# A sixth expert buffer, a new load order, a pairwise last iteration and a float32 gather in a two-layer transformer step

## What is computed

```python
# hierarchical MoE: top group, then top 2 of its 8 experts; 32 experts of width 256
hid = silu(einsum('bsd,edf->bsef', h, w_gate)) * einsum('bsd,edf->bsef', h, w_up)
hid = hid * combine[..., None]            # zero for experts that a token did not choose
y   = einsum('bsef,efd->bsd', hid, w_down)
x   = layer_norm(ALPHA * x + g2 * y, ln2_g, ln2_b)
```

## Time and profile before

| | |
|---|---|
| median of three runs | 1087.92 us |
| the profiled execution | 1086.85 us |
| its span | 1085.1 us |
| TensorE busy | 967.4 us (89%) |
| VectorE, ScalarE, GpSimd busy | 326.5, 230.6, 39.6 us |
| from HBM | 321.05 MB |
| expert gate and up loads | 64 of 2 MB, median 17.6 us from issue to landing |
| expert down loads | 64 of 1 MB, median 12.9 us |

### The profile page before, as it was taken

How to read it: one execution, slowest core, us unless ns; L and a number is a source line. 1 busy time by engine, 2 the same in 40 slices (tenths; PEclk the granted TensorE clock), 3 DMA queues, 4 the chain that set the end, 5 groups by cost and what they waited for, 6 DMA issues and landing times.

```text
span 1085.1 us, 15639 instructions
## 1 busy us (share of the span) xinstructions
PE 967.4 (89%) x6820; PEld 590.2 (54%) x6820; DVE 326.5 (30%) x744; ACT 230.6 (21%) x475; POOL 39.6 (4%) x60
## 2 busy tenths in 40 slices
PE   3999899998899898978879998999998989897875
PEld 1887758777743333334248876687884333332421
DVE  2112323222851312111170132331276231211215
ACT  2102314200251312111121132241014231211211
POOL 1100000010000000000010000000001000000000
PEclk9899999999999999998989999999999999999998
DMA  9938854586439999999875426766442999999970
GB/s 381 409 141 348 335 224 155 219 318 274 160 132 422 389 427 429 429 427 423 374 304 219 161 63 239 316 272 209 182 174 82 413 428 429 429 430 429 422 310 39
DMA packets 38526, 324.60 MB, mean 299 GB/s; under 512 B 4920, under 2 KB 5048, under 8 KB 9392
## 3 DMA queue, kind: packets, MB, share of 16 engines
q1 hardware_dynamic: 33696, 308.82, 69.6%
q0 software_dynamic: 4320, 13.28, 3.5%
q10 hardware_dynamic: 432, 1.39, 0.3%
HBM read 321.05 MB, written 2.42 MB: 298 GB/s over the span
## 4 chain that ended last, share of the span: by engine, by line
PE 75%; DMA 10%; DVE 6%; ACT 5%; issue 3%; SPq 1%; DVEq 0%; ACTq 0%
PE ps L768 13%; PE ps L666 9%; PE ps L817 8%; PE ps L692 6%; PE ps L872 5%; PE ps L944 5%; PE ps L958 5%; PE ps L781 5%; DMA expert_gate_up<-in_w_gu 4%; DMA expert_down<-in_w_dn 3%; PE ps L595 3%; PE ps L725 2%; PE ps L616 2%; DMA dense<-in_w_ada 2%; PE ps L827 2%
## 5 line engine op out<-in xcount | busy, mean ns | idle before, releaser
L768 PE MATMUL ps<-expert_gate_up,gathered_prompt 128*32 128x512 f32 x768 | 172.4, 603 | 5.0 <-ACT gathered_sample L1143 2.3
L768 PE MATMUL ps<-expert_gate_up,gathered_sample 128*32 128x512 f32 x768 | 172.4, 603 | 0.0
L817 PE MATMUL ps<-expert_down,hiddenT 128*32 128x512 f32 x1024 | 117.5, 602 | 11.8 <-ACT gathered_sample L1143 4.5
L666 PE MATMUL ps<-hT,dense 128*128 128x256 f32 x512 | 115.9, 385 | 0.0
L768 PEld LDWEIGHTS ps<-expert_gate_up,gathered_prompt 128*32 128x32 f32 x768 | 49.8, 111 | 115.6 <-issue 112.9
L666 PEld LDWEIGHTS ps<-hT,dense 128*128 128x128 f32 x512 | 97.4, 192 | 16.1 <-issue 2.8
L1557 DVE SCALAR_TENSOR_TENSOR y_lo<-ps,slot_weight,y_hi 128x512 fp32r<-128x512 f32 x64 | 48.1, 751 | 105.7 <-ACT y_hi L1175 105.6
L817 PEld LDWEIGHTS ps<-expert_down,hiddenT 128*32 128x32 f32 x1024 | 32.0, 110 | 82.8 <-issue 57.4
L1540 DVE TENSOR_TENSOR hidden<-hidden,ps 128x256 f32<-128x256 f32 x32 | 13.4, 420 | 194.0 <-ACT hidden L1159 194.0
L692 PE MATMUL ps<-dense,hT 128*128 128x256 f32 (+1 forms) x320 | 69.3, 381 | 1.7 <-ACT hT L1100 1.7
L692 PEld LDWEIGHTS ps<-dense,hT 128*128 128x128 f32 x320 | 60.6, 201 | 10.4 <-ACT hT L1100 2.5
(11 more groups left out here) (217 smaller groups left out, 1110.1 us busy)
## 6 DMA issues: line engine op xcount, KB each, us to landing
expert_gate_up<-in_w_gu SPq DMA_DIRECT2D x64, 2048.0 KB, 17.6
expert_down<-in_w_dn SPq DMA_DIRECT2D x64, 1024.0 KB, 12.9
dense<-in_w_ada SPq DMA_DIRECT2D x48, 1024.0 KB, 9.1
dense<-in_w_in SPq DMA_DIRECT2D x28, 1024.0 KB, 9.3
dense<-in_w_o SPq DMA_DIRECT2D x8, 1024.0 KB, 6.3
dense<-in_w_out SPq DMA_DIRECT2D x8, 1024.0 KB, 5.1
dense<-in_w_c SPq DMA_DIRECT2D x4, 1024.0 KB, 24.6
gate<-ada_rows POOLq DMA_DIRECT2D x4, 1024.0 KB, 8.5
```

Of the source, the lines that this page charges most:

```text
L666: last = mm(b[:, m * 256:(m + 1) * 256], w[:, k, m * P:(m + 1) * P], hT[:, k, :], start=(k == 0), stop=(k == KD - 1))
L768: last = mm(ps[r0:r0 + 32, q, :], xg[s][:, k, at_:at_ + CAP], w_gu[(i * EPI + 2 * q + j) % SLOTS][:, k, :], start=(k == 0), stop=(k == KD ...
L817: last = mm(ps[32 * e:32 * e + 32, banks[c], :], h, w_dn[(i * EPI + e) % SLOTS][:, f, c * 512:(c + 1) * 512], start=(f == 0), stop=(f == 1 ...
```

## The change

- A sixth expert buffer lies in the memory that held `h_hi` and `h_lo` (gate and up) and, for down, in that of `h2T`. Expert e lies in buffer e % 6, except 26 (buffer 5) and 29 (buffer 2). `gate2` and `ln2` move to the memory of buffer 5's gate and up part.
- The gather multiplies `xh2` itself by a float32 selection matrix, one matmul where there were two; `h_hi` and `h_lo` and their semaphores go.
- `gather_pair` uses banks 2, 3, 0, 1, and so also waits for the copies of `hiddenT` and `selectT` out of banks 0 and 1.
- The last iteration is done pairwise, as the middle ones; the down matmuls of request 1 are in two halves around the scatter of request 0, and VectorE's and ScalarE's programs follow.
- SP loads expert 5's gate and up after the attention (once `z_ready` is complete), its down part after expert 4's, then the others in a new order. `g2` and `ln2` are issued by SP behind the last expert.
- The first 15 dense loads of each layer go to other units (`FIRST_UNITS`).

```diff
-SLOTS = 5
+SLOTS = 6
+GATHER_BANK = (2, 3, 0, 1)
-FIRST_UNITS = (6, 7, 8, 9, 10, 12, 13, 0, 1, 3, 4, 11, 14, 2, 5)
+FIRST_UNITS = (9, 10, 11, 12, 13, 6, 7, 0, 1, 3, 4, 14, 8, 2, 5)
+BUFFER = [e % SLOTS for e in range(NE)]
+BUFFER[26], BUFFER[29] = 5, 2
...
# SP: load order
                     if (kind, i) == ("ada", gap_ada(l)[0] + 3):
+                        sp.wait_ge(z_ready, 8 * (l + 1))
+                        gate_up_load(l, M[l], 5)
                         first_gate_up(l, 3)
                         first_down(l, 3)
...
-                for e in range(5, EPI * 2):
-                    main_load(l, e)
-                for e in range(5, EPI * 2):
-                    main_down(l, e)
-                for i in range(2, ITERS):
-                    ...
+                k, v = nth(l, ("route", 1))
+                sp.wait_ge(filled[k], v + 1)
+                down_load(l, M[l], 5)
+                for e in range(6, 22, 4):
+                    for part in (e, e + 1, e + 2):
+                        main_load(l, part)
+                    for part in (e, e + 1):
+                        main_down(l, part)
+                    main_load(l, e + 3)
+                    for part in (e + 2, e + 3):
+                        main_down(l, part)
+                for e in (22, 23):
+                    main_load(l, e)
+                for e in (22, 23):
+                    main_down(l, e)
+                ... (the branch, then 24 and 25 in the same way)
+                for e in range(26, NE, 2):
+                    main_load(l, e)
+                    main_load(l, e + 1)
+                    main_down(l, e)
+                    main_down(l, e + 1)
+                sp.wait_ge(*reached(M[l], "h_filled", expert_pass(26)))
+                sp.wait_ge(ada_stored, 32 * (2 * l + 2))
+                load_rows(sp, l, 5, g2, post2_in)
+                load_ln(sp, l, "ln2", ln2, post2_in)
...
# TensorE: gather
-                    for hp, part in enumerate((h_hi, h_lo)):
-                        last = mm(ps[:, bank, at_ * CHUNK:(at_ + 1) * CHUNK], part[:, s, k * P:(k + 1) * P],
-                                  sel[:, n % 2, s, :], start=(hp == 0), stop=(hp == 1))
+                    last = mm(ps[:, bank, at_ * CHUNK:(at_ + 1) * CHUNK], xh2[:, s, k * P:(k + 1) * P],
+                              sel[:, n % 2, s, :], start=True, stop=True)
...
# TensorE: last iteration
-                gate_up_request(m, i, 0, 0, range(0, 8))
-                for s in range(2):
-                    scatter(m, i - 1, i - 1, s, False)
-                turn_request(m, i, 0, 0)
-                down(m, None, i, i, 0, (2, 3), False, ITERS + 1)
-                gate_up_request(m, i, 1, 1, range(0, 4))
-                scatter(m, i, i, 0, False)
-                gate_up_request(m, i, 1, 1, range(4, 8))
-                turn_request(m, i, 1, 1)
-                pe.wait_ge(*reached(m, "lo_done", 4 * i + 2))
-                down(m, None, i, i, 1, (2, 3), False, ITERS + 2)
-                scatter(m, i, i, 1, False)
+                for q in range(2):
+                    gate_up_pair(m, None, i, q)
+                    scatter(m, i - 1, i - 1, q, False)
+                turn_pairs(m, i)
+                down(m, None, i, i, 0, (2, 3), True, i + 2)
+                down(m, None, i, i, 1, (2, 3), True, i + 2, (0,))
+                scatter(m, i, i, 0, False)
+                down(m, None, i, i, 1, (2, 3), True, i + 2, (1,))
+                scatter(m, i, i, 1, False)
...
# VectorE: last iteration
-                hidden_product(m, i, 0, 0)
+                for q in range(2):
+                    hidden_product(m, i, q, q)
                 for c in range(2):
                     low(m, i, i, 0, c, 2 + c)
+                low(m, i, i, 1, 0, 2)
                 moe_sum(l, 0)
+                low(m, i, i, 1, 1, 3)
                 moe_residual(l, 0)
                 e = row_sums(y_sum, 0, 8, LN_EPS)
-                hidden_product(m, i, 1, 1)
                 centre(y_sum, ln2, 0)
-                low(m, i, i, 1, 0, 2)
                 scale(e, ln2, 0, 8, x2_ready, l)
-                low(m, i, i, 1, 1, 3)
```

More of the change, by code:

```diff
@@ L64 @@
 GAP_UNITS = (13, 14, 15, 12)
+BUFFER = [e % SLOTS for e in range(NE)]
+BUFFER[26], BUFFER[29] = 5, 2
+IN_BUFFER = [[e for e in range(NE) if BUFFER[e] == j] for j in range(SLOTS)]
 SMALL_LOADS = 6
@@ L363, in expert_pass, with load_rows, load_ln @@
             i = e // EPI
-            return 2 * i + 2 if i in (0, ITERS - 1) else 2 * i + (e % EPI) // 2 + 1
+            return 2 * i + 2 if i == 0 else 2 * i + (e % EPI) // 2 + 1
         def landed(r, e):
-            return 16 * (e // SLOTS + 1) if r is None else r * (16 * len(range(e % SLOTS, NE, SLOTS))) + 16 * (e // SLOTS + 1)
+            held = IN_BUFFER[BUFFER[e]]
+            n = 16 * (held.index(e) + 1)
+            return n if r is None else r * (16 * len(held)) + n
         def dram(ap, offset, dims):
             return bass.AP(ap.tensor, offset, dims)
+        def load_rows(eng, l, part, out, s):
+            src = dram(io["ada"], (l * 2 * ADA + part) * D, [[0, P], [ADA * D, 2], [1, D]])
+            eng.dma_start(out[:, :, :], src).then_inc(s, 16)
+        def load_ln(eng, l, name, out, s):
+            for j, n in enumerate((name + "_g", name + "_b")):
+                eng.dma_start(out[:, j, :], dram(io[n], l * D, [[0, P], [1, D]])).then_inc(s, 16)
         block = ctx.enter_context(nc.Block())
@@ L383, in dense_load @@
                 elif l and b < 15:
-                    e = max(range(b // 3, NE, SLOTS))
+                    e = IN_BUFFER[b // 3][-1]
                     if b % 3 < 2:
@@ L488, in store_rows @@
                     pool.dma_start(io["ada"][l, c, g], ada_row[c:P:32, :]).then_inc(ada_stored, 16)
-            def load_rows(l, part, out, s):
-                src = dram(io["ada"], (l * 2 * ADA + part) * D, [[0, P], [ADA * D, 2], [1, D]])
-                pool.dma_start(out[:, :, :], src).then_inc(s, 16)
-            def load_ln(l, name, out, s):
-                for j, n in enumerate((name + "_g", name + "_b")):
-                    pool.dma_start(out[:, j, :], dram(io[n], l * D, [[0, P], [1, D]])).then_inc(s, 16)
             def bias4_load(l, a, b):
@@ L800, in turn_request, with down @@
                 last.then_inc(w["hidT_filled"], 1)
-            def down(w, r, g, i, s, banks, paired, turns):
+            def down(w, r, g, i, s, banks, paired, turns, halves=(0, 1)):
                 if s == 0 or not paired:
                     for e in range(i * EPI, i * EPI + EPI):
-                        pe.wait_ge(*reached(w, "dn_in", landed(r, e), e % SLOTS))
+                        pe.wait_ge(*reached(w, "dn_in", landed(r, e), BUFFER[e]))
                     pe.wait_ge(*reached(w, "hidT_copied", turns))
-                for c in range(2):
+                for c in halves:
                     if paired and s:
```

118 lines of the change are left out of this document (54 added, 64 removed).

## The result

Four runs of the changed kernel took 1075.45, 1075.65, 1078.43 and 1080.28 us, median 1077.04; four of the kernel before took 1087.81 to 1088.95, median 1088.04. The ratio is 0.9909 [0.9891, 0.9926]: 8 to 12 us faster, where the forecast was 1083.2 us and its range began at 1079. Six more runs of the changed kernel later took 1079.12 to 1081.98 us (ratio 0.9935 [0.9915, 0.9955]); the median of all ten is 1080.2 us, against 1087.2 us for 59 runs of the kernel before. So the gain is nearer 7 than 11 us, and three us of the miss lie in which four runs came first: the six later ones all lie within the forecast's range.

A forecast was written before the change was run, and what follows sets the result against it. TensorE and the weight loads were taken to bound the kernel neck and neck. First layer +0.35 and second -5.0 gave -4.7 us: 1082.2 us profiled, 1083.2 us median; own range 1080.5 to 1086, wider range 1079 to 1089.

The forecast's parts named there:

- the price of the gathers: Float32 matmuls at 0.44 us: request 0's gather +0.5 (first layer) and 0, request 1's +1.1 us in each layer.
- the clock recovers further: Rival: request 0's gather has a hole shorter by 0.7 us and half clock behind it may not come; about 1080; chance 0.17.
- The closings: After down of iteration 6: 40.4 us in the first layer (-0.65), 43.2 in the second (-4.4).
- The hole before L703: Sign: in the first layer's closing TensorE stands idle for 8 to 9 us.
- Pair gathers: 16 float32 matmuls plus last readout take 8.1 us against 7.8 to 7.9: +0.25 us, twice a layer.
- After the branch: The gather there runs partly at half clock: 11.5 and 9.9 us, +1.8 in the first layer, +1.1 in the second.
- the wait at 469.24: First layer: TensorE's 1.2 us wait for a DMA goes, as TensorE comes later than the load lands.
- The clock's terms: Clock falls behind gathers go: first layer iteration 6 gate and up -1.7 us, second layer iteration 3 down -1.65.
- The loads: DMA waits shrink through new order and sixth buffer: -1.2 us in the first layer, -0.5 and -1.2 in the second.
- TensorE and the loads run neck and neck: Experts: 28.3 us an iteration on average against 29.3 of loads; additions to TensorE's path are paid almost in full.
- The free gather's time: Rival: readers, not TensorE, pace the float32 gather, so its added terms vanish; 1078.5 us; chance 0.08.
- The signs that would have shown the mechanism wrong: Gate and up wait in the last iteration, pair gathers over 9 us, or half clock through a whole gather.

The follow-up runs named there:

- e2: The kernel before with the pairwise last iteration alone; 1080.6 us, ratio 0.9943.
- e5: The kernel before with four banks for the pair gathers alone, float32r gather kept; 1082.52 us, ratio 0.9958.
- e12: The kernel before with four banks and the pairwise last iteration, float32r gather and five buffers kept; 1073.7 us, ratio 0.9863.
- e1: The kernel before with the float32 gather and four gather banks alone; 1086.86 us, ratio 1.0001.
- e3: The changed kernel with the old request-wise last iteration put back; 1073.12 us, ratio 0.9872.
- e4: The kernel before with float32 gather, four banks and pairwise last iteration, but five buffers, old loads and old FIRST_UNITS; 1079.98 us, ratio 0.9936.
- e6: The changed kernel with two banks instead of four for the pair gathers, float32 kept; 1084.74 us, ratio 0.9974.
- e7: The changed kernel run again, unaltered; 1080.64 us, ratio 0.9935.
- e9: The changed kernel with unused matmuls added, 12 ahead of the branch and 17 in the first layer's closing; 1078.09 us, ratio 0.9921.
- e10: e3 with unused matmuls added, 8 ahead of the branch and 5 in the first layer's closing; 1067.88 us, ratio 0.9825.
- e13: e12 with unused matmuls added, 8 ahead of the branch and 17 in the first layer's closing; 1068.96 us, ratio 0.9839.

## Why the prediction missed

The forecast by stages, as its own terms give it, beside the two profiled executions of the changed kernel (us, after less before):

```
                                forecast   first profile   second profile
to i=1, both layers               +2.7         +0.1            +0.1
first layer's loop                -0.6         -3.5            -1.5
second layer's loop               -1.7         +1.7            +1.1
closings, both layers             -5.05        -5.1            -5.1
dense stages                       0           -4.8            -0.8
```

- **The step that failed is the price of the gathers: it left out what their clock gives back.** The sum charged request 0's gather +0.5 us and request 1's +1.1 twice, and kept the half clock behind request 0's gather as it was: +2.7 us up to iteration 1. In all profiles of kernels with float32 gather these stages are 41.53 and 39.24 to 39.26 us, +0.1 in all. The stretches 298.45 to 302.01 at 0.52 and 818.86 to 822.13 at 0.80 now run at full clock (1.00 in the second and sixth stage above), worth 0.8 and 1.6 us, since request 1's gather in them did grow by 1.26. The rival "the clock recovers further", which had 0.17 and said 1080, came true where it was placed. In the kernel before, at this place, and in the changed one:

```profile
298.45 0.50 PE L725 MATMUL ps<-select,h_hi 128*128 128x256 f32 x1 [2.04 <-DVE gathered_prompt L1524]
...
300.04 1.97 PE L616 MATMUL ps<-const,x_hat 128*128 128x128 f32 x8
```

```profile
296.38 1.56 PE L750 MATMUL ps<-select,x_hat 128*128 128x256 f32 x6 [1.27 <-DVE gathered_prompt L1542]
297.97 1.09 PE L642 MATMUL ps<-const,x_hat 128*128 128x128 f32 x8
```

The hole went from 2.04 to 1.27 us, the 0.7 us of the rival. It is 2.04 us in e2, e5 and e12, with half clock behind it, and 1.27 in e1, e3, e4, e6 and e7, without. Longer matmuls and a shorter hole come together in every run, so which of the two keeps the clock up stays open.
- **The closings were right**: forecast 40.4 and 43.2 us, measured 40.43 and 43.15, in every kernel with this order (e2, e4, e6, e7, e12) within 0.05 us. Their terms, -0.65 and -4.4, are the -5.05 that e2 isolates at -6.2 [-8.2, -4.3] us by its ratio. The hole before L703 was forecast at 8 to 9 us and is 8.57.
- **The gathers' terms** one by one: request 1, +1.1, measured 3.65 - 2.39 = +1.26 us in both layers. Pair gathers: +0.25, measured +0.4. Request 0's: +0.5, measured 0 (5.29 us to the next instruction before and after). After the branch: +1.8 and +1.1, measured 0.0 and +2.2 in the first profile, +0.3 and +1.5 in the second. Gross forecast +6.6 us, measured 6.0 in e1's profile. With the clock (-3.35) and the wait at 469.24 (-1.2) e1's part of the forecast was +2.0; e1 took 1.0001 [0.9986, 1.0016], between -1.5 and +1.7 us, and 2.9 us of its profile are longer closings, which the forecast didn't have in this part.
- **The clock's terms, -1.7 and -1.65, were right for a wrong reason.** Gate and up of iteration 6 took 13.94 us instead of 15.64 in the first layer, as forecast, and the half clock in iteration 3 of the second layer is gone. But both falls, which I laid to the gather's holes, are missing in e2 too, which has the same gather: they stood in the one profiled execution of the kernel before and in none of the fourteen others. Iteration 6 took 18.03 us there from its first gate and up matmul to down, and 16.32 or 16.33 in every other profile and in its own second layer. The sum started from that very execution, so the terms fit; that is luck. e2 gave the time back in its second loop (185.53 us against 182.74): 4.2 us of waits for loads in place of 2.0, and 1.2 more in the gather after the branch. In the same way half clock at the start of iteration 1 of the first layer (0.79 over 8 us before and in twelve other profiles) was absent in the first profile of the changed kernel and in e3 (1.00), which is worth 1.7 us, and back in its second.
- **The mean granted clock** is 0.965 in the kernel before and in e2, 0.968 in e5 and e12, and 0.972 to 0.976 in every kernel with float32 gather and no added matmuls, e6 with its two banks (0.974) included. It goes with the float32 gather. That holes have no part in it is not shown: e6's are 0.25 us, those of before 0.64.
- **The loads were over-priced.** Forecast -1.2 in the first layer, -0.5 and -1.2 in the second. The wait at 469.24 went in e1 and e4 already, with five buffers: the longer gathers covered it, not the sixth buffer. And it was worth less than its 1.22 us: iteration 5 took 18.03 us from gate and up to down with it, 17.57 without. In the second layer e4 waits 0.54, 0.58 and 1.25 us, the changed kernel 1.15 us, near the place foretold (969.36; 978 in the old time). e4 against the changed kernel is a tie (1079.98 and 1080.2). I had costed the buffers beside a last iteration that no longer needs them, and didn't ask what they would be worth under the old one: 13.7 us.
- **"TensorE and the loads run neck and neck"** held, and told more than I drew from it: e5 makes TensorE 15.5 us shorter in the gathers and gains 4.7.
- **Readings and sums that were off without harm.** At 258 us the DMA was not idle: 255 to 262 moved 408 GB/s, and the 160 GB/s belong to the slice behind it. The pace of 24.6 us an iteration is the trace's (369.93 to 394.53), but the terms named give 23.4. The free gather's time is 1078.2 by its own terms, not 1078.5. The signs that would have shown the mechanism wrong didn't come: pair gathers took 8.29 us, no load was waited for in the last iteration, and the longest gather after the branch took 11.0 us, against 15.2 for one all at half clock.
- **The rest of the miss is chance, as far as the runs tell.** Of 11.7 us in the first profiled pair 4.8 lie in dense stages whose TensorE work is the same. Where no hole was filled, the dense stages range from 542.7 to 548.2 us, without regard to what was changed. The Trainium skill, page TensorE: Matmul & The Clock Gate (The HAM clock gate), says that the phase of the gate at a kernel's start differs from run to run. No run here shows the phase; they show executions of one kernel with other clocks and times (before: 1082.98 us at 0.968, 1089.99 us at 0.959, but also 1090.93 at 0.965). A forecast of the profiled execution to 2 us wasn't to be had, and my range ended 1.96 us above the median of four. It holds the median of all ten.

## What to carry over

Before you add two cures, make the table of two by two: when a wait has gone by the first, ask what the second still removes and what it costs, and time each alone and both. A hole removed and a matmul made longer can cancel to +0.4 us and look like one harmless edit of no cost; time them apart. A filled hole paid most where dense matmuls follow it directly, as behind the closing, and little ahead of a wait that stays, as at the branch. And see how far two profiles of one kernel differ before you take a term from one of them: both clock falls of this sum stood in a single execution.

## What the runs showed of the hardware that I had not expected

- Within one kernel the executions differ by up to 8 us (59 runs of the kernel before: 1082.98 to 1090.93), and about half of the variance goes with the mean granted clock, 0.959 to 0.970 (correlation -0.69).
- Float32 matmuls in the gather raise the mean granted clock by 0.005 over float32r ones (e5 to e1, e12 to e4). Four banks for two raise it by 0.003 with float32r (before to e5, e2 to e12), and not with float32 (e6 0.974, e7 0.972).
- With 8 or 12 matmuls in front of the branch TensorE still stands idle for 2.5 to 3.0 us behind it (e9 2.71 and 2.83, e10 2.98 and 2.48, e13 2.6 twice). The profile names VectorE's `select`, which stands behind a branch as well, as what ended some of these, and nothing for the others. In e10 the 2.98 us are followed by half clock in the gather (0.84 over 10.57 us).
- Matmuls into a free bank, whose result nobody reads, made both best versions faster by 5 us (1073 to 1067.9 and, with overlapping intervals, 1073.7 to 1069.0), and of that some 3 lie in the dense stage behind the filled closing. At the branch they took 0.6 and 1.1 us off in e13, which its loops did not keep.
